# One triangular inverse for both directions, the first projection from unnormalised input, and reordered dilated and merge steps

## The reference, cut to what matters

```
h    = rmsnorm(x) * ln_mix_pre
proj = h @ w_in                          # all projections of the layer
qkv  = silu(conv5(proj[q, k, v]))        # depthwise over time, 5 taps, 3072 channels
g    = -exp(a_log) * softplus(a + dt);   beta = sigmoid(b)      # per token and head, forward and backward
o_a  = delta(q, k, v, g_f, beta_f) + flip(delta(flip q, flip k, flip v, g_b, beta_b))
o_a  = rmsnorm(o_a) * silu(z)
o_b  = three dilated groups of biased windowed attention, mixed by their log sums
y    = (sigmoid(ga) * (o_a @ w_branch_a) + sigmoid(gb) * (o_b @ w_branch_b)) @ w_out
```

## Time and profile before

| what | value |
|---|---|
| median of 3 runs | 2108.91 us (2108.44 to 2112.96) |
| the profiled execution's own time | 2110.14 us |
| span in the trace | 2108.3 us |
| mean granted TensorE clock | 0.972 |
| TensorE busy | 1998.5 us, 95% |
| VectorE, ScalarE, GpSimd busy | 940.0, 743.6, 614.7 us |

### The profile page before, as it was taken

The page is one execution under the profiler, slowest core; times in us unless marked ns, Lnnn a source line. Parts: engine busy times, 40 slices in busy tenths (PEclk is TensorE's granted clock), DMA queues, the critical chain, the costliest instruction groups (busy, mean ns, idle before and its releaser), DMA issues.

```text
span 2108.3 us, 25286 instructions
## 1 busy us (share of the span) xinstructions
PE 1998.5 (95%) x10748; PEld 1607.1 (76%) x10748; DVE 940.0 (45%) x1549; ACT 743.6 (35%) x1235; POOL 614.7 (29%) x206
## 2 busy tenths in 40 slices
PE   6998899999999999999999999998999999999997
PEld 3777899999977787778778888887766548766456
DVE  4797455656522221303336403514534664434663
ACT  4674232221433322322233212223343553343551
...
GB/s 170 60 80 60 1 1 2 2 1 1 95 120 105 106 90 76 111 84 91 89 80 82 98 100 100 100 99 61 130 60 80 1 1 83 90 60 80 1 1 40
DMA packets 29001, 142.01 MB, mean 67 GB/s; under 512 B 2871, under 2 KB 7351, under 8 KB 14808
## 3 DMA queue, kind: packets, MB, share of 16 engines
q1 hardware_dynamic: 18944, 123.27, 16.5%
...
...
## 4 chain that ended last, share of the span: by engine, by line
PE 86%; DVE 7%; ACT 4%; issue 1%; DMA 0%; POOL 0%; SPq 0%; POOLq 0%; DVEq 0%; ACTq 0%
PE bank L398 48%; PE bank L942 13%; PE bank L599 4%; PE bank L409 3%; PE bank L1800 3%; PE bank L1821 3%; PE bank L1807 2%; DVE WK L868 2%; PE bank L957 2%; PE bank L1275 1%; DVE WK L887 1%; PE bank L1251 1%; PE bank L1749 1%; ACT WK L1930 1%; ACT w_part L356 1%
## 5 line engine op out<-in xcount | busy, mean ns | idle before, releaser
L398 PE MATMUL bank<-x_part,w_part 128*128 128x512 f32 x3360 | 786.7, 394 | 3.5 <-ACT WK L1497 3.0
L398 PEld LDWEIGHTS bank<-x_part,w_part 128*128 128x128 f32 x3360 | 633.1, 189 | 141.5 <-issue 9.0
L2240 POOL TENSOR_TENSOR w_part<-RAW,w_part 128x2048 fp32r<-128x2048 f32 (+1 forms) x90 | 403.3, 4484 | 780.1 <-ACT w_part L356 777.7
L942 PE MATMUL bank<-WK 128*128 128x64 f32 (+1 forms) x2336 | 281.2, 277 | 3.4 <-DVE WK L1088 1.6
L942 PEld LDWEIGHTS bank<-WK 128*128 128x128 f32 x2336 | 275.7, 195 | 4.3 <-DVE WK L1088 1.8
L2240 POOL TENSOR_TENSOR w_part<-WK,w_part 128x2048 fp32r<-128x2048 f32 (+1 forms) x30 | 126.2, 4206 | 376.5 <-ACT w_part L356 376.5
L356 ACT ACTIVATE w_part<-RAW 128x2048 fp32r<-128x2048 f32 (+1 forms) x90 | 166.4, 1850 | 173.9 <-PE bank L398 138.3
L398 PE MATMUL bank<-f_part,w_part 128*128 128x512 f32 x768 | 174.4, 389 | 0.0
L398 PEld LDWEIGHTS bank<-f_part,w_part 128*128 128x128 f32 x768 | 144.2, 188 | 29.9
L868 DVE SCALAR_TENSOR_TENSOR WK<-WK,COL 128x512 f32<-128x512 f32 x96 | 101.7, 1060 | 3.4
L1009 ACT ACTIVATE WK<-bank 128x256 f32<-128x256 f32 x80 | 31.0, 388 | 200.9 <-PE bank L957 200.6
...
## 6 DMA issues: line engine op xcount, KB each, us to landing
...
```

Of the source, the lines that this page charges most:

```text
L398: mm = pe.eng.matmul(b[:, :], W[w][:, k, c:c + P], src[x][k], start=start and k == 0 and n == 0, stop=stop and k == kn - 1 and n == 2)
L942: mul = lambda o, a, b: E.matmul(o, a, b, start=True, stop=True)
L2240: eng.tensor_tensor(low_part(i), raw_part(i), high_part(i).bitcast(F32), ALU.subtract).then_inc(w_split, 1)
```

## The change

What it does, in the order of the program:

1. **First projection.** VectorE makes split operands `UX` from x times its gain, without the norm. TensorE multiplies the four tiles of A0 by them right after the sum of squares (both tiles of a piece are interleaved over the contraction), and VectorE multiplies these four tiles in PSUM by the row factor afterwards (`rowed`). The gates are projected after the first tile of A1. ScalarE rounds piece 0 after all squares, piece 1 after the row factor, piece 2 between the second and third slice of the normalised operand.
2. **Convolution.** ScalarE writes the middle tap from PSUM, VectorE adds four taps reading PSUM, 510 or 511 wide. `XP`, its zeroing and the fifth VectorE instruction go. Gate work moves two tiles later.
3. **One inverse for both directions.** 8 units of (chunk, half) take the place of 16. beta goes into the decay's exponent, so that both directions share one matrix A (lower half forward, upper half backward), one K K' and one Q K'. Products of a level are 128 wide, 64 columns for each direction; the transpose is shared too, but for the last. Units start at the slots in `START`, and the steps of the state follow as chunks are ready. Storage moves, some of it into the raw weight buffer.
4. **After the gdn stage.** The first two pieces for the z gate are rounded by ScalarE and GpSimd after all their gdn work.
5. **Dilated.** v0 is projected before the first logits, the transposes of v come before `logits(n + 2)` and `logits(n + 3)`.
6. **Merge.** TensorE's barrier at its start goes, the first two gates are passed through the sigmoid in `dil`, WB's tiles are merged in PSUM, and each low part follows its tile.

The core of the diff ("..." marks what is left out; `step` holds the five state products as before):

```diff
+            ahead(upto=1)
             for k in range(KO):
                 act.wait_ge(*at((nm, "tmp", k)))
                 act.eng.activation(XH[0][:, k, :], norm_mem(nm)[2][:, k % 2, :], ACT.Copy).then_inc(*act.did((nm, "hi", k)))
+                if k == 1:
+                    ahead(upto=2)
...
+            for p in range(2):
+                bs = [job(("qkv", 0, 2 * p + j)) for j in range(2)]
+                hi, lo = (w.rearrange("p (k n) -> p k n", n=256) for w in (high_part(p), low_part(p)))
+                pe.wait_ge(*at(("hi", p)))
+                for k in range(KO):
+                    pe.wait_ge(*at(("ux", k)))
+                    for j, b in enumerate(bs):
+                        for x in range(2):
+                            pe.eng.matmul(b[:, :], hi[:, k, j * P:(j + 1) * P], UX[x][:, k, :], start=k == 0 and x == 0, stop=False)
+                pe.wait_ge(*at(("split", p)))
+                for j, b in enumerate(bs):
+                    for k in range(KO):
+                        mm = pe.eng.matmul(b[:, :], lo[:, k, j * P:(j + 1) * P], UX[0][:, k, :], start=False, stop=k == KO - 1)
+                    mm.then_inc(*pe.did(("pe", ("qkv", 0, 2 * p + j))))
+                used(p)
+
...
-            act_norm("n1", XT, need=arrived, before_sum=lambda: ahead(upto=1))
+            act_norm("n1", XT, need=lambda k: [(x_in[k // 2], 16)], before_sum=lambda: ahead(upto=0))
...
+            for k in range(KO):
+                dve.wait_ge(x_in[k // 2], 16)
+                g = col("ln_mix_pre", k)
+                dve.eng.tensor_scalar(UX[0][:, k, :], XT[:, k, :], g, None, ALU.mult).then_inc(*dve.did())
+                dve.wait_ge(*dve.last())
+                dve.eng.scalar_tensor_tensor(out=UX[1][:, k, :], in0=XT[:, k, :], scalar=g, in1=UX[0][:, k, :].bitcast(F32),
+                                             op0=ALU.mult, op1=ALU.subtract).then_inc(*dve.did(("ux", k)))
...
-                act.eng.activation(XP[:, n % 2, 2:S + 2], ps(("qkv", c, i))[:, :], ACT.Copy)\
-                    .then_inc(*act.did(("xp", n), free=("qkv", c, i)))
+                    act.wait_ge(*at(("si", *tiles[n - 2])))
+                act.eng.activation(CV[:, n % 2, :], ps(("qkv", c, i))[:, :], ACT.Copy, scale=col("conv", n * CONV + 2))\
+                    .then_inc(*act.did(("cv", n)))
...
+            def rowed(i):
+                dve.wait_ge(*at(("pe", ("qkv", 0, i))))
+                V.tensor_tensor(ps(("qkv", 0, i))[:, :], ps(("qkv", 0, i))[:, :], RSB, ALU.mult).then_inc(*dve.did(("rowed", i)))
...
-                V.tensor_scalar(cv, XP[:, n % 2, 0:S], wc(0), None, ALU.mult).then_inc(*dve.did())
-                for j in range(1, CONV):
-                    dve.wait_ge(*dve.last())
-                    V.scalar_tensor_tensor(out=cv, in0=XP[:, n % 2, j:j + S], scalar=wc(j), in1=cv, op0=ALU.mult,
-                                           op1=ALU.add).then_inc(*dve.did(*([("conv", n)] if j == CONV - 1 else [])))
+                if n < 3:
...
+                cv, x = CV[:, n % 2, :], ps(("qkv", c, i))
+                for j, (to, at_, m) in ((0, (2, 0, S - 2)), (1, (1, 0, S - 1)), (3, (0, 1, S - 1)), (4, (0, 2, S - 2))):
+                    if j:
+                        dve.wait_ge(*dve.last())
+                    V.scalar_tensor_tensor(out=cv[:, to:to + m], in0=x[:, at_:at_ + m], scalar=wc(j), in1=cv[:, to:to + m], op0=ALU.mult,
+                                           op1=ALU.add).then_inc(*dve.did(*([("conv", n)] if j == CONV - 1 else []),
+                                                                          free=("qkv", c, i) if j == CONV - 1 else None))
...
+        units = [(c, hf) for c in (0, 3, 1, 2) for hf in range(2)]
+        unit_of = {x: u for u, x in enumerate(units)}
+        START = (0, 1, 2, 3, 12, 13, 19, 20)
+        INVERSE = 17
...
+        def begin(s, gi):
+
+            d, hf = groups[gi]
+            at_ = START[unit_of[chunk_of(d, s), hf]] + INVERSE
+            return max(at_, begin(s - 1, gi) + 3) if s else at_
...
+            def invert(u, ph):
+                c, hf = units[u]
                 tok = slice(c * P, (c + 1) * P)
-                g = WRKG[gi]
-                mul = lambda o, a, b: E.matmul(o, a, b, start=True, stop=True)
+                A, UC, PB = a_of(u), uc_of(u), product(u)
                 if ph == 0:
-                    four("gr", s, gi, lambda o, h: mul(o, Gg[:, c, k0 + h:k0 + h + 1].broadcast_to([P, P]), tri(d)))
+                    for d in range(2):
+                        four(("gr", u, d), lambda o, h: mul(o, Gg[:, c, 8 * d + 4 * hf + h:8 * d + 4 * hf + h + 1].broadcast_to([P, P]), tri(d)))
                 elif ph == 3:
-                    four("qk", s, gi, lambda o, h: mul(o, KF[:, 4 * hf + h, tok], QF[:, 4 * hf + h, tok]))
-                    four("kk", s, gi, lambda o, h: mul(o, KF[:, 4 * hf + h, tok], KF[:, 4 * hf + h, tok]))
+                    four(("kk", u), lambda o, h: mul(o, KF[:, 4 * hf + h, tok], KF[:, 4 * hf + h, tok]))
+                    four(("qk", u), lambda o, h: mul(o, KF[:, 4 * hf + h, tok], QF[:, 4 * hf + h, tok]))
                 elif ph == 4:
-                    pe.wait_ge(*at(("abar", s, gi)))
-                    four("p0", s, gi, lambda o, h: E.transpose(o, g[A_][:, h, :], ident))
-                elif ph in LEVELS:
+                    pe.wait_ge(*at(("a", u)))
+                    four(("p", u, 0), lambda o, h: E.matmul(o, A[:, h, :], split_ident, start=True, stop=True, is_transpose=True), half_of)
+                elif ph >= 5:
                     l, update = level(ph)
                     if not update:
-                        if l > 1:
-
-                            pe.wait_ge(*at(("t", s, gi, l - 1)))
-                            four(f"ut{l - 1}", s, gi, lambda o, h: E.transpose(o, g[T_][:, h, :], ident))
-
-                        pe.wait_ge(*at(("t", s, gi, l - 1)))
-                        four(f"p{l}", s, gi, lambda o, h: mul(o, g[A_][:, h, :], halves(g[T_][:, h:h + 1, :], 1 << l, d)), 64)
+                        pe.wait_ge(*at(("t", u, l - 1)))
+                        if l == 1:
+                            pe.wait_ge(*at(("kept", u)))
+                        four(("p", u, l), lambda o, h: mul(o, A[:, h, :], t_open_of(u, l, h)), half_of)
+                        if l == 6:
+                            for d in range(2):
+                                four(("ut", u, 5, d), lambda o, h: E.transpose(o, t_heads(u, d)[:, h, :], ident))
+                        elif l > 1:
+                            pe.wait_ge(*at(("mixed", u, l - 1)))
+                            four(("ut", u, l - 1), lambda o, h: E.transpose(o, UC[:, h, :], ident))
+                    elif l < 6:
+                        pe.wait_ge(*at(("u", u, l - 1)))
+                        pe.wait_ge(*at(("pm", u, l)))
+                        four(("tu", u, l), lambda o, h: mul(o, UC[:, h, :], PB[:, :, h, :]), half_of)
                     else:
-                        pe.wait_ge(*at(("pm", s, gi, l)))
-                        pe.wait_ge(*at(("u", s, gi, l - 1)))
-                        if l < 6:
-                            four(f"tu{l}", s, gi, lambda o, h: mul(o, g[U_][:, h, :], halves(g[P_][:, h:h + 1, :], 1 << l, d)), 64)
-                        else:
-                            pe.wait_ge(*at(("pz", s, gi)))
-                            four(f"tu{l}", s, gi, lambda o, h: mul(o, g[P_][:, h, :], halves(g[U_][:, h:h + 1, :], 1 << l, 1 - d)), 64)
-                        if l == 6 and s:
-                            pe.wait_ge(*at(("state", s - 1, gi)))
-                            four("ks", s, gi, lambda o, h: mul(o, KF[:, 4 * hf + h, tok], ST[:, gi, h, :]))
-                elif ph == 17:
+                        pe.wait_ge(*at(("u", u, 5)))
+                        pe.wait_ge(*at(("pm", u, 6)))
+                        b = job(("tu", u, 6))
+                        for h in range(4):
+                            for d, (lo, off) in ((0, (0, 64)), (1, (64, 0))):
+                                mm = mul(b[lo:lo + 64, h * 64:h * 64 + 64], PB[:, 1 - d, h, :], inverse(u, d)[:, h, off:off + 64])
+                        mm.then_inc(*pe.did(("pe", ("tu", u, 6))))
...
+            for gi in range(4):
+                act.wait_ge(*at(("pe", ("ov", 2, gi))))
...
+                elif ph == 3:
+                    pool.wait_ge(*at(("gam", u, 0)))
+                    pool.wait_ge(*at(("gam", u, 1)))
+                    if u >= 6:
+                        pool.wait_ge(*at(("pe", ("ds", 0, u - 6))))
+                    G.tensor_tensor(A, qm(u, 0), qm(u, 1), ALU.add).then_inc(*pool.did(("decay", u)))
                 elif ph == 4:
-                    pool.wait_ge(*at(("abar", s, gi)))
-                    G.tensor_tensor(g[U_], g[A_], b4(lev(0, 1 - d)), ALU.mult).then_inc(*pool.did())
+                    pool.wait_ge(*at(("n0", u)))
```

(20 more changed lines are left out.)

505 lines of the change are left out of this document (300 added, 205 removed).

## The result

The median is 1965.85 us (1964.58 to 1968.18, 4 runs) against 2108.77 (2108.44 to 2112.96, 4 runs) on the same chip: ratio 0.9319, 95% interval 0.9303 to 0.9335. Predicted were 1973, and 1952 to 2003.

The account below looks back on a forecast made before the run. TensorE, busy 95% of the span, was taken to bound the kernel. Gains of 21 (load and qkv), 91 (gdn) and 25 us (dilated and merge) sum to 137, taking 2110 to 1973 us, range 1952 to 2003.

Parts of the forecast that it names:

- Term 1: Load and qkv: earlier A0 and fewer TensorE waits gain 21 us, bounds 12 and 25.
- The 4.7 us for the gate decays: Load and qkv: TensorE's 4.7 us wait for gate decays goes because they move two tiles later.
- Term 2: gdn: 1856 records instead of 2848 plus waits, 243 us against 333.6, gains 91 us, bounds 66 and 107.
- the last level's price: gdn, last level's `tu`: 128 narrow records taken at 0.11 us each, 14 us; LDWEIGHTS rule would give 0.055 each.
- end with GpSimd's T or transposed copy: gdn's start: TensorE's waits end with these GpSimd results, its 24 instructions taking 30.5 us; 22 us lost with half clock.
- Term 3: Dilated and merge: waits for v copies, k slices and at the merge's ends go, 25 us, bounds 14 and 26.
- Covered, barely at worst: Dilated: first probabilities, with 11 us instead of 16.5 after v0's move, still come in time; engines need some 7.
- each follows its tile by some 2.8 us: Merge's end: low parts come this soon after their tiles, so the 4.4 us wait goes.
- (a): Rival: gdn keeps the low clock at both ends, stage 278 us, total 2008 us; chance 0.13.
- (c): Rival: in gdn a 128-wide product of two strided runs costs as two, adding 77 us, total 2050; chance 0.03.
- (d): Rival: TensorE at half clock for the whole gdn stage, 447 us, total 2177 us, slower; chance 0.02.
- (b): Rival: everything goes well, gdn starts at full clock, last level at half price or less, total 1946; chance 0.07.

Follow-up runs that it names:

- conv_alone: The kernel before with only the change's convolution (taps read PSUM, no padded copy), without the move of gate work: 2097.23 us, ratio 0.9949 to the kernel before.
- masks_first: The changed kernel with GpSimd's masks and decay sums for all units ahead of transposed copies in each slot of the inverse: 1948.77 us.
- vector_masks: all_three with VectorE instead of GpSimd adding the masks of the first four units (8 instructions): 1933.60 us.
- late_operand: The changed kernel with A0 again projected from the normalised operand, old load order and gates in front, convolution kept: 1981.40 us.
- third_late: The changed kernel with ScalarE rounding the third weight piece behind the eight slices of the normalised operand, not amid them: 1972.55 us.
- round_last: The changed kernel with ScalarE's rounding of the next merge weight piece behind that of the merged half, not ahead: 1962.09 us.
- old_dil: The changed kernel with the old orders of TensorE (in part), ScalarE and VectorE in the dilated attention: 1983.91 us.
- all_three: The changed kernel with masks_first, round_last and an earlier ScalarE rounding of the first two z-gate pieces together: 1935.89 us.
- the split runs: Each 128-wide inverse product issued as two 64-wide ones, on the changed kernel (2064.77 us) and on masks_first (2027.92 us).

## Why the prediction held, point by point

**Term 1, 21 us; measured 28.7 (above its bound of 25).** The start of A0 (17, was 16.26), the end (40, was 38.4) and the gates behind A1's first tile are right; the 14.0 came out as 15.4. Two steps failed. "The 4.7 us for the gate decays go, since they move two tiles later": they go, but conv_alone shows that the convolution alone does it. And the half clock behind that wait was never in the sum: 5.1 − 2.6 for the sums and 7.8 − 5.75 for a tile, 4.6 us. The new wait of the first head sums (1.5) didn't come. The squares' 3.1 went as said, and 0.4 instead of 0.7 ahead of the transposes.

**Term 2, 91 us; measured 95.5, and 1.5 given back in the z gate.** The step that failed is the last level's price, for which I took 0.11 against the rule. By form, in gdn:

```profile
L1032 PE MATMUL bank<-WK 128*64 128x64 f32 x112 | 5.5, 228 | 0.0
```

With 16 more in another group (1.4 us) these 128 records take 6.9 us, 0.054 each, and not 14. By the Trainium skill ("TensorE: Matmul & The Clock Gate", section on LDWEIGHTS) a load of 64 weight columns takes half the time of one of 128, and the trace agrees. The wide ones are as forecast (eight in 0.89 us): 1728 x 0.111 + 6.9 = 199 against 204. Around them: start 48 us (184 to 232) with 256 records, 28 us of work, so 20 lost against 22; the slots where units 6 and 7 open 6 (12 us from 316 to 328 with 56 records) against 3; end 3.7 of waits and some 2 of half clock against 6; z gate 5.3 + 1.5 against 8. That leaves some 3 us in gdn that I assign to nothing.

A second step had the path wrong. The waits at the start were to "end with GpSimd's T or transposed copy", set by GpSimd's amount, 30.5 us. Only 0.7 us of them did; 8.4 us ended with VectorE's L1237, which stood for GpSimd's decay sum. GpSimd owned the start through its order: masks_first has the same 24 instructions. With that order the wait left (4.0) ends with T, and taking 8 of the 24 away (vector_masks) is worth 2 us more.

Part of the agreement is luck. The same gdn code takes 238.1 us in three profiles (after, late_operand, third_late) and 232.9 and 233.0 in two (round_last, old_dil), by its share of half clock; the profiled execution of the kernel after is the slowest of its four. Between after and round_last the 5.2 us arise in three places: 1.3 in the start, 2.4 where units 6 and 7 open, 1.5 ahead of the z gate.

**Term 3, 25 us; measured 19.9.** The waits for copies of v, for the k slices and at the merge's start went, and old_dil gives the order its 16.6 us. "Covered, barely at worst" held for the probabilities: their transposes (L1423) wait for nothing. Three things took from the term. The first is the new wait of the logits, 0.35 us in each head group, 1.4 in all. The second is more half clock in the first head group. The first 37 us of the stage, of before, after, old_dil and all_three:

```profile
596.58:633.58 37.00, 37.00 (x129) 25.85 (x130) 4.46 (x7) 14.28 (x27) 10.07 (x3) 0.91 0.34 128
```
```profile
473.87:510.87 37.00, 37.00 (x115) 25.58 (x116) 4.46 (x7) 14.26 (x27) 9.76 (x3) 0.82 0.33 128
```
```profile
470.74:507.74 37.00, 37.00 (x115) 25.64 (x116) 4.46 (x7) 14.28 (x27) 9.82 (x3) 0.82 0.33 128
```
```profile
450.91:487.91 37.00, 37.00 (x143) 26.21 (x144) 4.46 (x7) 14.87 (x28) 10.08 (x3) 1.00 0.32 128
```

0.82 against 0.91 costs some 3 us. old_dil has it with the old order, and all_three has none of it, so it comes from what runs ahead of the stage and not from the new order; how is open. The third is the merge's end, where the 4.4 became 2.4 and not 0: "each follows its tile by some 2.8 us" overlooked ScalarE's 1.9 us weight rounding ahead of it, which round_last shows.

The errors, +7.7, +3.0 (4.5 − 1.5) and −5.1, less the 0.7 behind the merge, make 4.9 of the 7 us between 1973 and 1965.85. They partly cancel. The rest is the 2.3 us by which the profiled execution (1968.18) lies above the median.

**Sums.** Four of the prediction's sums don't come out. Term 2's lower bound, 333.6 − 278, is 56 and not 66. Term 1's, 21.0 − 7 − 3.1, is 11 and not 12. The half clock at the merge's start, 12.62 − 48 x 0.23, is 1.6 and not 1.7. And 1993, "the terms' own bounds", takes gdn at its forecast of 91; with its lower bound it is 2110 − (12 + 56 + 14) = 2028. So the upper end of the range, 2003, is a choice that leaves (a) outside, and not what the terms' bounds give. The measured time lies inside either.

**Rivals.** (c) is excluded by the split runs: if the merged call cost as two, splitting it would have cost nothing. (a) is excluded by the last slots, 380 to 420, which were granted 0.94 on the whole, and (d) by the stage's mean of 0.93. Of (b) one half came true, the last level at half price; the start was not at full clock (0.80 from 184 to 232), and gdn's 95.5 lies nearer to the forecast's 91 than to its 114.
